# Three groups per neighbourhood step, and latent chunks begun inside the differential drain

## The chip, the cores and the metric

The kernel runs on one core of a Trainium2 chip. It is one program in which five engines work through queues of their own: TensorE (matrix products and transposes, results in PSUM), VectorE, ScalarE, GpSimd, and SyncE, which issues most transfers. They wait for each other by semaphores alone. The metric is the device time of one execution in microseconds (us).

## What is computed

The reference is two blocks, one behind the other, over 1024 tokens of width 1024. The first block has two layers of three kinds of attention each; both layers hold the code that is changed. The second block (state space mixer, stick-breaking attention, pooling, MLP) is untouched. Cut to what matters:

```python
def hybrid_layer(x, ...):                      # twice
    proj = (rms_norm(x) * (1 + scale) + shift) @ w_in
    # latent heads: 6 heads, queries and keys of 64 + 32 (rotated) from latents of 256 and 128
    q = rms_norm((rms_norm(c_q) @ w_uq)), k = rms_norm(concat(k_nope, k_pe)), rope on the last 32
    o_mla = softmax(q k^T * 96**-0.5) @ v_mla                       # 1024 x 1024 per head
    # neighbourhood heads: 6 heads of 64; tokens are a 16 x 64 grid, each sees 8 x 16 neighbours
    o_na = softmax(qn kn^T * 64**-0.5 + rpb, neighbours only) @ vn
    # differential heads: 4 heads, two score maps of 32 each
    a = softmax(q0 k0^T) - lam * softmax(q1 k1^T)
    o_d = rms_norm(a @ vd) * (1 - lam_init)
    y = concat(o_mla * silu(g_mla), o_na * silu(g_na), o_d * silu(g_diff)) @ w_out
    return x + gate * y
```

## The kernel before

A layer runs in five stages: projection, neighbourhood heads, differential heads, latent heads, output. Tokens lie along the free axis, 128 partitions hold features or, for score tiles, 128 queries. PSUM has eight banks of 512 columns, here `ps[:, 0..7]`.

**Neighbourhood stage.** 24 steps: three pairs of heads (`hp`) by eight tiles of 128 queries (`t`, `NA_PAIRS`). A step works on both heads of a pair (`j`), so unit `u` is `2 s + j`. Tiles 2 to 5 of each pair are inner ones, with 576 keys; the others have 512. TensorE forms the scores of both heads (`scores`, L1415, head 0 in banks 0 and 1, head 1 in 2 and 3). VectorE adds the bias and takes the maximum (`top`, L3160), then negates it (L3165). ScalarE exponentiates (`exps`, L2249). TensorE transposes the probabilities, four blocks of 128 keys and for inner tiles one of 64 (`probs_t`, L1429, always banks 4 and 5), ScalarE copies them out of PSUM (`evacuate`, L2259) and VectorE the block of 64 for the odd head (L3172). TensorE multiplies by the values (`values_of`, L1445, bank 6), VectorE copies the result (`out`, L3177). TensorE's order in step s is: transposes of unit 2s-1, scores of step s+1, transposes of unit 2s, values of step s-1. When a pair of heads is through, VectorE takes reciprocals of its sums (L3208), GpSimd spreads them (`na_wide`, L3833), TensorE transposes them in two halves in steps 11, 12, 19 and 20 (`factors`, L1458, bank 7), and VectorE multiplies (`out_times`, L3186). From step 10 to 19 VectorE also does one operation per step of the rotation of the latent keys (`key_rope`). In step 24 the first differential scores are formed, and then a barrier follows.

**Differential stage.** 32 units, two per tile of 128 queries. In iteration c TensorE forms the two score maps of unit c (L1477, banks 0 and 1, 2 and 3), does half of a value product (L1524, banks 6 and 7), and transposes unit c-2 (L1535, banks 4 and 5). VectorE takes maxima (L2927), a reciprocal (L3223), the difference of the two maps (L3230) and the out (L3236); ScalarE exponentiates (L2267) and copies the transposes (L2296); GpSimd forms one ratio per unit (L3844). Iterations 32 to 35 drain the pipeline. Into the drain are put four of eight latent value products (`latent_v`, L1219, copied by ScalarE, L2102), the factor transposes of the third neighbourhood pair, and the square of the first differential pair (ScalarE, L2303). Then comes a barrier (`phase_end`).

**Latent opening.** Queries and keys of a pair of heads are made in eight chunks of 256 columns (`LAT_CHUNKS`); the first six (`LAT_AHEAD`) come ahead of the first scores. A chunk goes: product on TensorE (`latent_main`, L1133 and L1136, bank p % 4), squares on ScalarE (L2060), their sum on GpSimd (`squares_sum`, L3862), sum over features on TensorE (`latent_sums`, L1143), root on ScalarE (L1895 and L1897), scaling on VectorE (`latent_scaled`, L2921 and L2955), rounding on ScalarE (L2075, L2082), low parts on VectorE (`latent_low`, L2966) and GpSimd (`turned_low`, L3869). Before the chunks TensorE makes the other four value tiles; GpSimd squares the second differential pair (L3864). Behind the chunks TensorE does the first two differential sums (L1209, L1211, banks 6 and 7), and then the first latent scores (L1160, L1167), which need chunks 0 to 4 ready and all six scaled.

The waits that hold the order around the change are these (TensorE, `latent`):

```python
pe.wait_ge(sems["lat_v_done"], NT * layer + 4 + min(p, 3) + 1)
if p >= 4:
    pe.wait_ge(sems["lat_used"], LAT_C * layer + p - 3)
latent_main(layer, p, p % 4)
if p:
    pe.wait_ge(sems["lat_v_done"], NT * layer + NT)
    if p >= 3:
        pe.wait_ge(sems["lat_rstd"], LAT_C * layer + p - 2)
    latent_sums(layer, p - 1, 4 + (p - 1) % 2, 0)
```

## Time and profile before

| | us |
|---|---|
| median of 3 timed runs (3835.05 to 3836.61) | 3835.8 |
| the profiled execution | 3830.2 |
| its span, first to last instruction | 3828.2 |
| TensorE busy | 3752.3 |
| VectorE busy | 2660.5 |
| ScalarE busy | 1927.6 |
| GpSimd busy | 643.5 |

In the profile a busy TensorE is not TensorE at its peak: matrix products are pipelined, and the row of weight loads (PEld, 2924.3 us) shows gaps that the row of products hides. "issue" is time in which an engine waited for nothing that the profile shows. The two layers take the first 1740 us or so; the two show the same pattern. A line number is that of the instruction in the kernel before.

### The profile page before, as it was taken

The numbers are of one execution on the slowest core, as the hardware profiler recorded it, in microseconds if no ns is written. First come the engines' busy times: TensorE is split into PE (matmuls) and PEld (weight loads), VectorE is DVE, ScalarE is ACT, GpSimd is POOL, SyncE is SP. The second block draws the span as 40 slices with busy tenths as digits, with TensorE's granted clock in tenths as the row PEclk, the third lists the DMA queues.
The fourth block names the chain that finished last, engine by engine and source line by source line (L and its number), as shares of the span: only waits on it lengthen the run. The fifth ranks groups of instructions, "written<-read, shape, count | busy, mean of one in ns | idle before, by whom it ended". The sixth has DMA issues, their size and how long they took to land.

```text
span 3828.2 us, 53662 instructions
## 1 busy us (share of the span) xinstructions
PE 3752.3 (98%) x21588; PEld 2924.3 (76%) x21588; DVE 2660.5 (69%) x3337; ACT 1927.6 (50%) x2841; POOL 643.5 (17%) x723
## 2 busy tenths in 40 slices
PE   8999999999999999999999999999999999999999
PEld 5876667887876667887853778888888888888887
DVE  4347967675347967534456745988889869888898
ACT  5337866324337866324357444453545554535454
POOL 0120121001120121011049911000001420000010
PEclk9999999999999999999999999999999999999999
DMA  5332000453232000332100011211121201111111
GB/s 212 94 97 54 1 1 12 176 212 108 94 97 54 1 1 13 121 118 71 45 23 1 26 45 66 78 44 44 57 76 45 77 13 67 55 44 55 67 55 66
DMA packets 67734, 247.54 MB, mean 65 GB/s; under 512 B 15648, under 2 KB 16288, under 8 KB 55456
## 3 DMA queue, kind: packets, MB, share of 16 engines
q1 hardware_dynamic: 53648, 193.51, 15.0%
q10 hardware_dynamic: 13840, 50.60, 3.6%
q8 instruction: 172, 2.82, 0.3%
q14 instruction: 74, 0.61, 0.1%
HBM read 206.34 MB, written 29.36 MB: 62 GB/s over the span
## 4 chain that ended last, share of the span: by engine, by line
PE 85%; DVE 5%; ACT 4%; issue 2%; POOL 2%; DMA 1%; DVEq 0%; SPq 0%; ACTq 0%; POOLq 0%
PE ps L1788 32%; PE ps L1045 13%; PE ps L1297 3%; PE ps L1299 3%; PE ps L1298 3%; PE ps L1477 2%; PE ps L1160 2%; PE ps L1193 2%; PE ps L1579 2%; PE ps L1524 2%; PE ps L1535 2%; PE ps L1429 2%; DMA w<-in_wstream 1%; PE ps L1445 1%; PE ps L1415 1%
## 5 line engine op out<-in xcount | busy, mean ns | idle before, releaser
L1788 PE MATMUL ps<-x_piece1hi,w_piece1hi 128*128 128x512 f32 x672 | 262.4, 390 | 0.2 <-DVE x_piece1lo L3529 0.2
L1788 PE MATMUL ps<-x_piece0hi,w_piece0hi 128*128 128x512 f32 x672 | 262.3, 390 | 0.0
L1788 PE MATMUL ps<-x_piece0hi,w_piece0lo 128*128 128x512 f32 x672 | 261.5, 389 | 0.0
L1788 PE MATMUL ps<-x_piece1hi,w_piece1lo 128*128 128x512 f32 x672 | 261.4, 389 | 0.0
L1788 PE MATMUL ps<-x_piece0lo,w_piece0hi 128*128 128x512 f32 x672 | 261.4, 389 | 0.0
L1788 PE MATMUL ps<-x_piece1lo,w_piece1hi 128*128 128x512 f32 x672 | 261.4, 389 | 0.0
L1788 PE MATMUL ps<-x_piece2hi,w_piece2lo 128*128 128x512 f32 x672 | 261.4, 389 | 0.0
L1788 PE MATMUL ps<-x_piece2hi,w_piece2hi 128*128 128x512 f32 x672 | 261.4, 389 | 0.0
L1788 PE MATMUL ps<-x_piece2lo,w_piece2hi 128*128 128x512 f32 x672 | 261.4, 389 | 0.0
L1045 PE MATMUL ps<-n_hi_m,w_lo 128*128 128x512 f32 x576 | 225.5, 391 | 0.0
L4047 POOL TENSOR_TENSOR rope_cos<-rope_cos,arena 128x512 f32<-128x512 f32 x42 | 65.4, 1557 | 730.4 <-ACT arena L2496 727.3
L2988 DVE TENSOR_REDUCE small<-ps 128x1 f32<-128x1024 f32 x96 | 113.0, 1219 | 78.7 <-PE ps L1167 78.5
L2927 DVE TENSOR_REDUCE small<-ps 128x1 f32<-128x1024 f32 x128 | 154.2, 1212 | 15.3 <-PE ps L1477 15.3
L2267 ACT ACTIVATE h<-ps,small 128x1024 f32<-128x1024 f32 x128 | 142.7, 1115 | 37.0 <-DVE small L2927 36.9
L4047 POOL TENSOR_TENSOR rope_sin<-rope_sin,arena 128x512 f32<-128x512 f32 x28 | 45.2, 1615 | 640.7 <-ACT arena L2496 638.3
L2550 ACT ACTIVATE m<-m 128x1024 f32<-128x1024 f32 x80 | 85.0, 1062 | 131.9 <-DVE m L3573 103.9
L1788 PEld LDWEIGHTS ps<-x_piece1hi,w_piece1hi 128*128 128x128 f32 x672 | 126.1, 188 | 27.2 <-DVE x_piece1lo L3529 0.6
L1788 PEld LDWEIGHTS ps<-x_piece0lo,w_piece0hi 128*128 128x128 f32 x672 | 126.1, 188 | 26.6 <-issue 0.5
L1788 PEld LDWEIGHTS ps<-x_piece1lo,w_piece1hi 128*128 128x128 f32 x672 | 126.1, 188 | 26.6 <-issue 0.5
L1788 PEld LDWEIGHTS ps<-x_piece0hi,w_piece0hi 128*128 128x128 f32 x672 | 126.1, 188 | 26.6 <-DVE w_piece1lo L3522 0.2
L1788 PEld LDWEIGHTS ps<-x_piece1hi,w_piece1lo 128*128 128x128 f32 x672 | 126.1, 188 | 26.3
L1788 PEld LDWEIGHTS ps<-x_piece0hi,w_piece0lo 128*128 128x128 f32 x672 | 126.1, 188 | 26.2
(515 smaller groups left out, 10652.3 us busy)
## 6 DMA issues: line engine op xcount, KB each, us to landing
w<-in_wstream SPq DMA_DIRECT2D x87, 1024.0 KB, 5.0
arena<-in_wstream SPq DMA_DIRECT2D x40, 1024.0 KB, 4.9
arena<-in_wstream ACTq DMA_DIRECT2D x16, 1024.0 KB, 5.3
n_saved<-n_hi_m SPq DMA_DIRECT2D x16, 512.0 KB, 7.3
n_saved<-n_lo SPq DMA_DIRECT2D x16, 512.0 KB, 8.2
n_hi_h<-n_saved SPq DMA_DIRECT2D x16, 512.0 KB, 8.2
n_lo<-n_saved SPq DMA_DIRECT2D x16, 512.0 KB, 9.2
out<-h ACTq DMA_DIRECT2D x32, 256.0 KB, 2.3
```

Of the source, the lines that this page charges most:

```text
L1045: last = mm(dst, a_part[:, k, wcols], b_part[:, tile0 + k, :], start=(k == 0 and b_part is hi and a_part is wb[0]), stop=(k == nk - 1 and ...
L1160: mm(ps[:, 2 * j + hf, :], lt_split(hp, 0, q, r)[a_part], lt_split(hp, 1, keys, r)[b_part], start=(part == 0), stop=False)
L1193: last = mm(ps[64 * j:64 * j + 64, 6, 0:P], lt_v[:, b, hp * P + 64 * j:hp * P + 64 * j + 64], lt_pt_of(2 * s + j)[:, b * P:b * P + P], sta ...
L1297: mm(dst, wb[0][:, k, wcols], hi[:, k, :], start=(step == 0), stop=False)
L1298: mm(dst, wb[0][:, k, wcols], lo[:, k, :], start=False, stop=False)
L1299: last = mm(dst, wb[1][:, k, wcols], hi[:, k, :], start=False, stop=(step == KT - 1))
L1788: last = mm(dst[:, e, :], a_part[:, pair, k, f], b_part[:, k, :], start=(n in FRESH and half == 0 and k == 0 and t == 0), stop=(half == 1 ...
L2267: nc.scalar.activation(df_p[:, 2 * (c % 3) + i, :], psf[:, 2 * i * HALF:(2 * i + 2) * HALF], ACT.Exp, bias=negm[:, e:e + 1], accum_out=sum ...
L2550: nc.scalar.activation(x, x, ACT.Square if st.kind == "up" else ACT.Sigmoid).then_inc(sems["unit_done"], 1)
L2927: V.reduce_max(negm[:, u:u + 1], src, AX.X, negate=True).then_inc(sems["m_ready"], 1)
L2988: V.reduce_max(negm[:, u:u + 1], psf[:, 2 * j * HALF:(2 * j + 2) * HALF], AX.X, negate=True)\
L4047: G.tensor_tensor(out=x, in0=x, in1=ring[:, r % 2, :], op=ALU.add).then_inc(sems["t_added"], 1)
```

## The change

In the neighbourhood stage TensorE's step becomes: scores of step s+1, transposes of both heads of step s, values of step s-1. The even head's transposes go to bank 4, the odd head's to bank 7, the 64-key blocks of both to bank 5. ScalarE copies bank 4 and the small blocks, VectorE copies bank 7. The maximum is taken negated, so that the negation goes; the exponential takes scale -1. Factors move to steps 14, 15, 22, 23 and to bank 5. The first differential scores move from step 24 to step 23.

The barrier between differential and latent stage goes. Chunks 0 to 3 and the first sums are put into iterations 32 to 35, the value products between and behind them, one bank (6) and later two (6 and 7), copied by VectorE. The squares of both differential pairs go to GpSimd, the first into its loop behind unit 20, the second between chunks 4 and 5.

```diff
@@ tiles
+        na_pt_odd, at = region(arena, lt_end + 2 * NA_INNER, NA_K)
         def df_pt_of(v):
-            return (df_pt1 if v // 2 % 2 else df_pt0)[:, v % 2, :]
+            return (df_pt0 if v // 2 % 2 else df_pt1)[:, v % 2, :]
+        LAT_SUM_PLACE = ((1, LAT_W), (1, LAT_W), (2, LAT_W), (5, 0), (4, 0), (5, 0))
+        def lat_v_bank(t):
+            return 7 if t >= 4 and t % 2 == 0 else 6
@@ SyncE, bias of the third pair
-                sp.wait_ge(sems["t_done"], 6 * layer + 2)
+                sp.wait_ge(sems["lat_rs"], 2 * LAT_PAIRS * layer + 1)
@@ TensorE, latent
             def latent_v(layer, t):
-                if t in (2, 3, 4, 5):
-                    pe.wait_ge(sems["lat_v_done"], NT * layer + t - 1)
-                mm(ps[:, t % 2 if t < 4 else t - 4, 0:384], lt_kv[:, t * P:t * P + P], lt_wv, start=True, stop=True)\
+                if t:
+                    pe.wait_ge(sems["lat_v_done"], NT * layer + (t if t < 4 else t - 1))
+                mm(ps[:, lat_v_bank(t), 0:384], lt_kv[:, t * P:t * P + P], lt_wv, start=True, stop=True)\
                     .then_inc(sems["lat_v_full"], 1)
+            def latent_opening_sums(layer, p):
+                if p == LAT_AHEAD - 1:
+                    pe.wait_ge(sems["lat_rstd"], LAT_C * layer + p - 1)
+                latent_sums(layer, p, *LAT_SUM_PLACE[p])
             def latent(layer):
-                for t in range(4, NT):
+                for p in (4, 5):
+                    pe.wait_ge(sems["lat_used"], LAT_C * layer + p - 3)
+                    latent_main(layer, p, p % 4)
+                    latent_opening_sums(layer, p - 1)
+                for t in (3, 4, 5):
                     latent_v(layer, t)
...
+                latent_opening_sums(layer, 5)
+                for t in (6, 7):
+                    latent_v(layer, t)
+                pe.wait_ge(sems["lat_v_done"], NT * layer + NT)
                 for i in range(2):
                     differential_sums(layer, i)
@@ TensorE, neighbourhood
+                    def probs_t(s):
+                        hp, t, _, inner = NA_PAIRS[s]
+                        pe.wait_ge(sems["exp_done"], T.since("exp_done", 2 * s + 2))
+                        if s:
+                            pe.wait_ge(sems["pt_act"], T.since("pt_act", s))
...
+                        for j in range(2 if inner else 0):
+                            nc.tensor.transpose(ps[0:GW, 5, j * P:j * P + P], na_p_of(2 * s + j)[:, NA_W:NA_INNER], ident)
+                        for j in range(2):
+                            if s and j:
+                                pe.wait_ge(sems["pt_dve"], T.since("pt_dve", s))
+                            for b in range(NA_W // P):
+                                last = nc.tensor.transpose(ps[:, 7 if j else 4, b * P:b * P + P],
+                                                           na_p_of(2 * s + j)[:, b * P:b * P + P], ident)
+                            last.then_inc(sems["t_full"], 1)
                     for s in range(NA_STEPS + 1):
-                        if s == NA_STEPS:
+                        if s + 1 < NA_STEPS:
+                            scores(s + 1)
+                        elif s + 1 == NA_STEPS:
...
                             for i in range(2):
                                 df_scores(0, i)
-                        if s:
-                            probs_t(2 * s - 1)
-                        if s + 1 < NA_STEPS:
-                            scores(s + 1)
-                        if s < NA_STEPS:
-                            probs_t(2 * s)
                         if s == 0:
                             keep_busy(7, 8)
+                        if s < NA_STEPS:
+                            probs_t(s)
                         if s:
                             values_of(s - 1)
-                        if s > NT and s % NT in (3, 4):
-                            factors(s // NT - 1, s % NT - 3)
+                        if s in NA_FACTORS_AT:
+                            factors(*NA_FACTORS_AT[s])
@@ TensorE, differential drain
+                        if c == U:
+                            pe.wait_ge(sems["lat_w"], 128 * (layer + 1))
+                            pe.wait_ge(sems["exp_done"], T.since("exp_done", 2 * U - 1))
+                            for p in range(2):
+                                latent_main(layer, p, p)
+                        if c == U + 1:
+                            pe.wait_ge(sems["lat_sq"], LAT_SQUARES[-1] * layer + LAT_SQUARES[1])
+                            latent_opening_sums(layer, 0)
                         if c >= 4:
...
-                        if c in (U - 1, U + 1):
-                            for v in range(2):
-                                latent_v(layer, 2 * (c > U) + v)
...
+                        if c == U + 1:
+                            pe.wait_ge(sems["na_m_done"], T.since("na_m_done", 2))
+                            for p in (2, 3):
+                                latent_main(layer, p, p)
+                            pe.wait_ge(sems["lat_rstd"], LAT_C * layer + 1)
+                            latent_opening_sums(layer, 1)
+                            pe.wait_ge(sems["o_free"], T.since("o_free", DF_STEPS - 1))
+                            latent_v(layer, 0)
+                        if c >= U + 2:
+                            latent_v(layer, c - U - 1)
+                        if c == U + 2:
+                            latent_opening_sums(layer, 2)
+                    pe.wait_ge(sems["o_free"], T.since("o_free", DF_STEPS))
-                phase_end()
@@ ScalarE
+            def latent_opening(layer, p):
+                if p < LAT_AHEAD:
+                    for part in range(2 - LAT_CHUNKS[p][1]):
+                        latent_squares(layer, p, p % 4, part)
+                if p:
+                    latent_root(layer, p - 1, *LAT_SUM_PLACE[p - 1])
+                if p >= 2:
+                    latent_high(layer, p - 2)
+                if p >= 3:
+                    turned_high(layer, p - 3)
...
+                        for j in range(2 if NA_PAIRS[s][3] else 0):
+                            nc.scalar.activation(na_pt_of(2 * s + j)[0:GW, NA_W:NA_K], ps[0:GW, 5, j * P:j * P + P], ACT.Copy)
+                        nc.scalar.activation(na_pt_of(2 * s)[:, 0:NA_W], ps[:, 4, :], ACT.Copy).then_inc(sems["pt_act"], 1)
+                    exps(0)
+                    exps(1)
+                    for s in range(NA_STEPS):
+                        evacuate(s)
+                        if s + 1 < NA_STEPS:
+                            exps(2 * s + 2)
+                            exps(2 * s + 3)
...
-                        if c in (U, U + 2):
-                            for v in range(2):
-                                latent_v(layer, 2 * (c > U) + v)
-                        if c == U + 1:
-                            act.wait_ge(sems["o_free"], T.since("o_free", NT))
-                            nc.scalar.activation(m[:, 0, :], m[:, 6, :], ACT.Square).then_inc(sems["lat_d_act"], 1)
+                        for p in {U: (0,), U + 1: (1,), U + 2: (2,)}.get(c, ()):
+                            latent_opening(layer, p)
-                phase_end()
@@ VectorE
+            def latent_v(layer, t):
+                dve.wait_ge(sems["lat_v_full"], NT * layer + t + 1)
+                V.tensor_copy(lt_v[:, t, :], ps[:, lat_v_bank(t), 0:384]).then_inc(sems["lat_v_done"], 1)
             def latent(layer):
...
+                latent_scaled(layer, 3, 3)
+                latent_v(layer, 2)
+                latent_low(layer, 2)
+                latent_scaled(layer, 4, 0)
+                latent_v(layer, 3)
+                latent_low(layer, 3)
+                latent_v(layer, 4)
+                latent_scaled(layer, 5, 1)
+                latent_low(layer, 4)
+                latent_v(layer, 5)
+                latent_low(layer, 5)
+                for t in (6, 7):
+                    latent_v(layer, t)
...
-                            na_inner[hp][:, j, :] if inner else na_bias[hp % 2][:, j, e * GW:e * GW + NA_W], 1.0, 4 * MASKED, ALU.add, ALU.max, mx[:, u:u + 1])\
-                            .then_inc(sems["v_link"], 1)
-                        dve.wait_ge(sems["v_link"], T.next("v_link"))
-                        V.tensor_scalar(negm[:, u:u + 1], mx[:, u:u + 1], -1.0, None, ALU.mult)\
+                            na_inner[hp][:, j, :] if inner else na_bias[hp % 2][:, j, e * GW:e * GW + NA_W], -1.0, -4 * MASKED, ALU.add, ALU.min, negm[:, u:u + 1])\
                             .then_inc(sems["m_ready"], 1)
+                    def probs_t(s):
+                        dve.wait_ge(sems["t_full"], T.since("t_full", 2 * s + 2))
+                        if s >= 2:
+                            dve.wait_ge(sems["o_full"], T.since("o_full", s - 1))
+                        V.tensor_copy(na_pt_of(2 * s + 1)[:, 0:NA_W], ps[:, 7, :]).then_inc(sems["pt_dve"], 1)
...
+                        if c == U + 2:
+                            latent_scaled(layer, 1, 1)
+                            latent_low(layer, 0)
+                            latent_v(layer, 0)
+                        if c == U + 3:
+                            latent_scaled(layer, 2, 2)
+                            latent_low(layer, 1)
+                            latent_v(layer, 1)
                         if c >= 5 and c % 2:
...
+                            latent_scaled(layer, 0, 0)
+                            latent_turned(layer, 0, 0)
+                            latent_turned(layer, 0, 1)
-                phase_end()
@@ GpSimd
+                    if v == DF_STEPS + 4:
+                        pool.wait_ge(sems["o_free"], (NA_STEPS + DF_STEPS + LAT_STEPS) * layer + NA_STEPS + NT)
+                        G.tensor_tensor(out=m[:, 0, :], in0=m[:, 6, :], in1=m[:, 6, :], op=ALU.mult).then_inc(sems["lat_d_sq"], 1)
+                    for p in range(2 if v == DF_U - 1 else 0):
+                        squares_sum(p)
-                phase_end()
-                G.tensor_tensor(out=m[:, 1, :], in0=m[:, 7, :], in1=m[:, 7, :], op=ALU.mult).then_inc(sems["lat_d_act"], 1)
-                for p in range(LAT_AHEAD):
+                for p in range(2, LAT_AHEAD):
                     squares_sum(p)
                     if p >= 3:
                         turned_low(p - 3)
+                    if p == LAT_AHEAD - 2:
+                        pool.wait_ge(sems["o_free"], (NA_STEPS + DF_STEPS + LAT_STEPS) * layer + NA_STEPS + DF_STEPS)
+                        G.tensor_tensor(out=m[:, 1, :], in0=m[:, 7, :], in1=m[:, 7, :], op=ALU.mult).then_inc(sems["lat_d_sq"], 1)
```

## Rows read from the trace of the kernel before

**Rows 1.** Table of stretches: us, busy by engine (instructions), granted clock, DMA share, GB/s.

```profile
484.00:513.20 29.20, 23.44 (x156) 16.89 (x152) 13.78 (x28) 17.08 (x43) 12.87 (x15) 1.00 0.00 0
1344.00:1373.50 29.50, 23.73 (x158) 17.19 (x157) 13.99 (x28) 17.37 (x44) 13.06 (x15) 1.00 0.00 1
```

**Rows 2.** Chain of waits, an inner neighbourhood step: start us, us, what.

```profile
283.98 0.70 PE ps L1429 x5
284.67 1.23 PE ps L1415 x8
285.90 0.69 PE ps L1429 x5
286.60 1.39 PE ps L1445 x20
```

**Rows 3.** Timeline, TensorE's weight loads: start us, us, engine, line, shapes, count, idle before.

```profile
480.67 0.86 PEld L1535 LDWEIGHTS ps<-mats,h 128*128 128x128 f32 x8 [0.17 <-issue]
481.58 0.94 PEld L1219 LDWEIGHTS ps<-arena 128*128 128x128 f32 x4
...
714.79 1.02 PEld L1201 LDWEIGHTS ps<-mats,arena 128*128 128x128 f32 x8
```

**Rows 4.** Chain of waits, the neighbourhood stage's second, last and next scores.

```profile
273.60 1.23 PE ps L1415 x8
...
352.78 1.06 PE ps L1415 x4
...
363.49 0.52 PE ps L1477 x3
```

**Rows 5.** Groups by shape, 268 to 362: count, busy us, mean ns, idle before.

```profile
L2259 ACT ACTIVATE h<-ps 128x512 f32<-128x512 f32 x30 | 17.9, 597 | 17.0 <-PE ps L1429 17.0
L2249 ACT ACTIVATE h<-h,small 128x576 f32<-128x576 f32 x12 | 9.2, 768 | 0.0
...
L3165 DVE TENSOR_SCALAR small<-small 128x1 f32<-128x1 f32 x48 | 7.4, 154 | 1.7
L3160 DVE CUSTOM_DVE_ANT_0 h<-ps,w 128x576 f32<-128x576 f32 x8 | 6.1, 758 | 3.4 <-PE ps L1415 2.7 <-DVE h L2937 0.7
L3172 DVE COPY h<-ps 64x128 f32<-64x128 f32 x12 | 3.4, 282 | 2.1 <-PE ps L1429 1.9
L3186 DVE TENSOR_TENSOR m<-m,ps 128x512 f32<-128x512 f32 x4 | 2.7, 687 | 1.1 <-PE ps L1458 1.1
```

**Rows 6.** Latent opening: chain pieces, timeline pieces and groups by shape of single operations.

```profile
476.44 0.34 POOL L3844 TENSOR_SCALAR small<-small,lam 128x1 f32<-128x1 f32 x1 [3.37 <-DVE small L3223]
...
492.61 2.82 PE ps L1219 x8
492.65 1.89 POOL L3864 TENSOR_TENSOR m<-m 128x1024 f32<-128x1024 f32 x1 [6.47 <-DVEq L2700]
...
504.29 0.42 DVE L2966 TENSOR_TENSOR w_lo<-w,lt_high 128x256 fp32r<-128x256 f32 x1
...
508.88 0.67 PE L1143 MATMUL ps<-h,mats_r 128*128 128x256 f32 x2 [1.06 <-POOL h L3862]
...
509.38 0.87 POOL L3869 TENSOR_TENSOR lt_high<-arena,lt_k_turned 128x256 fp32r<-128x256 f32 x1 [0.65 <-ACT lt_k_turned L2082]
509.58 0.95 DVE L2966 TENSOR_TENSOR w_lo<-w,lt_high 128x256 fp32r<-128x256 f32 x1
509.55 0.86 PE ps L1209 x2
510.00 0.42 ACT L1897 ACTIVATE h<-h 128x256 f32<-128x256 f32 x1
...
513.18 1.66 PE ps L1160 x12
...
L2966 DVE TENSOR_TENSOR w_lo<-w,lt_high 128x256 fp32r<-128x256 f32 x6 | 4.5, 756 | 0.0
L2921 DVE SCALAR_TENSOR_TENSOR w<-ps,c_tmp,h 128x256 f32<-128x256 f32 x6 | 2.9, 476 | 0.6 <-ACT h L1897 0.6
```

More of the change, by code:

```diff
@@ L510 @@
 NA_MASKS = 33 + 32
-NA_INNER_AT = [sum(x[3] for x in NA_PAIRS[:s]) for s in range(NA_STEPS + 1)]
+NA_FACTORS_AT = {NT * (hp + 1) + NT - 2 + hf: (hp, hf) for hp in range(NA_H // 2 - 1) for hf in range(2)}
 DF_UNITS = [(hp, j, t) for hp in range(DF_H // 2) for t in range(NT) for j in range(2)]
@@ L3202, in _ @@
                             top(2 * s + 3)
+                        elif s + 1 == NA_STEPS:
+                            for i in range(2):
+                                maximum(i, psf[:, 2 * i * HALF:2 * i * HALF + 2 * HALF], NA_STEPS)
+                        if s < NA_STEPS:
+                            probs_t(s)
                         if s:
@@ L3231, in _ @@
                                 .then_inc(sems["a_done"], 1)
+                        if c == U:
+                            for hf in range(H2):
+                                dve.wait_ge(sems["t_done"], T.since("t_done", hf + 1))
+                                out_times(LAT_PAIRS - 1, hf, 2 + hf)
+                        if c == U + 2:
[6 more added lines that the diff above has]
+                            latent_v(layer, 1)
                         if c >= 5 and c % 2:
@@ L3832, in na_wide @@
                 def na_wide(hp):
-                    G.tensor_copy(na_wides[hp].rearrange("p t (j d) -> p (t j) d", j=2),
-                                  rs[:, 16 * hp:16 * hp + 16].unsqueeze(2).to_broadcast([P, 16, 64])).then_inc(sems["lat_wide"], 1)
+                    for hf in range(H2):
+                        last = G.tensor_copy(na_wides[hp][hf].rearrange("p t (j d) -> p (t j) d", j=2),
+                                             rs[:, 16 * hp + 8 * hf:16 * hp + 8 * hf + 8].unsqueeze(2).to_broadcast([P, 8, 64]))
+                    last.then_inc(sems["lat_wide"], 1)
                 for hp in range(LAT_PAIRS - 1):
@@ L3839, in _, with squares_sum @@
                 phase_end()
+                def squares_sum(p):
+                    quarter = LAT_CHUNKS[p][2]
+                    pool.wait_ge(sems["lat_sq"], LAT_SQUARES[-1] * layer + LAT_SQUARES[p])
+                    x = lt_sq[:, p % 2, 0, :]
+                    other = pe_sq[:, quarter * LAT_W:quarter * LAT_W + LAT_W] if LAT_CHUNKS[p][1] else lt_sq[:, p % 2, 1, :]
+                    G.tensor_tensor(out=x, in0=x, in1=other, op=ALU.add).then_inc(sems["lat_sum"], 1)
                 pool.wait_ge(sems["lat_rs"], 2 * LAT_PAIRS * layer + LAT_PAIRS)
```

143 lines of the change are left out of this document (37 added, 106 removed).

## Prediction

> **What bounds the kernel now.** I first read the table of stretches: which engine is busy in which stage. Each of the two layers holds the same two stretches that the change touches, the neighbourhood stage (about 268 to 362 in layer 0) and the opening of the latent heads, from the last differential unit to the first latent scores (484 to 513 in layer 0, 1344 to 1373.5 in layer 1). In the opening TensorE has work for 23.4 of 29.2 us, VectorE for 13.8, ScalarE for 17.1, GpSimd for 12.9, all at the full granted clock [rows 1]: no engine is the bound, a chain across engines is. Then I read the chain of waits in the neighbourhood stage. It consists of TensorE alone, group after group without a gap: the odd head's transposes, scores, the even head's transposes, values. An inner step (576 keys; twelve of the 24) takes 0.70 + 1.23 + 0.70 + 1.39 = 4.02 us [rows 2]; an edge step (512 keys) has the same four groups without the pieces of 64 keys. So this stage gains only by what TensorE no longer does or no longer waits between groups. Last I read the weight loads, which show those gaps: a group of eight transposes loads weights for 0.86 us, and 0.17 passes before it begins after a group of another kind [rows 3].
>
> Everything is worked out for layer 0 and doubled. Sums are made against the profiled execution, 3830.2 us (span 3828.2 and 2.0 around it); the median of the timed runs is 3835.8, 5.6 above, and I lay the difference on that.
>
> **The neighbourhood step.** Four groups become three; the number of transposes stays. Two groups of four in a row pay the change of kind once: 0.17 saved. Against it stands a new wait between them, for the VectorE copy of the step before. Waits between groups of the same kind are in the trace: eight differential transposes end at 481.53 and the latent value products behind two waits start at 481.58, a gap of 0.05; the eight factor transposes at 714.79 have a wait in the middle and take 1.02 rather than 0.86 in all, of which the slow product ahead explains a part [rows 3]. The wait costs 0 to 0.16; I take 0.05, the direct gap. Saved per step 0.12, over the 21 steps from the scores at 273.60 to the last scores at 352.78 [rows 4]: 2.5 us.
>
> Does another engine become late? ScalarE now copies one head (0.60) and, in inner steps, two pieces of 64x128; the trace has no such copy on ScalarE, so I bound it between 0.2 and the 0.60 of 128x512, and take 0.2, since 0.60 is for four times the elements. VectorE copies the other head: 0.69 like the product of that size, and loses the negation, 0.15 twice, and the small copy of 0.28. VectorE's inner step is then two maxima of 0.76, a copy of 0.69 and the out, about 0.3 for as many columns as the small copy [rows 5], some 2.6 of 3.9 us, with a turning operation of 0.7 in ten steps: covered. If that cover were gone, every us would delay the next scores directly. Scale -1 in the maximum and in the exponential changes no duration.
>
> The factor transposes move from steps 11, 12, 19, 20 to 14, 15, 22, 23. A group of four costs half of the 0.86 of eight on TensorE [rows 3]. The last two now stand behind the last scores, where VectorE is late anyway (two maxima of the differential scores, the copy, two outs): 0.9 saved. The differential scores come one step earlier: from the last scores to the first differential scores behind the barrier it takes 10.7 us now [rows 4]; in the new order TensorE needs 3.9 to the differential scores, VectorE then 0.9 + 2.4 + 0.7 + 0.3, TensorE the last values 1.0, VectorE 0.6, and the barrier 0.3, together 10.1: 0.6 saved. At the start the negation leaves the way to the second scores: 0.2. Sum 2.5 + 0.9 + 0.6 + 0.2 = **4.2 us saved per layer**, between 1.9 (the wait costs 0.16) and 5.2 (nothing).
>
> **Cheap edits.** The third bias load waits for the reciprocals of step 8 rather than the factors of step 12; its three transfers go out earlier on SP's queue, and the swaps behind it wait for the end of the stage as before: 0, and were it late, the scores of head pair 2 would wait. The square of the first differential pair goes from ScalarE's drain into GpSimd's loop, 1.89 us, where GpSimd idles 3.4 us between two ratios [rows 6]: 0; above 3.4 it would hold up a differential unit one for one. The two differential tiles that change places cost nothing.
>
> **The opening.** Removed are a barrier, the ScalarE copies of eight latent value tiles, and a square on ScalarE. The copies go to VectorE: 384 columns, between 0.28 (128 columns) and 0.69 (512) [rows 5], in proportion 0.55 each. The chunks start at 481.6, when the transposes of unit 29 are through, rather than at 495. But the new queues tie the chunks together:
>
> TensorE waits for the squares of chunk 1 before the first sums. Those squares stand on ScalarE behind the copy of unit 30, so they end at 487.4; behind TensorE's wait stand the last differential values and transposes, for which ScalarE's and VectorE's copies wait. Then follow sums 0.67, values 1.02, transposes 1.02, two latent products 0.9, sums 0.67: 491.6. The root of chunk 1 (0.84) ends at 492.5.
>
> From here value tiles 1 and 2 are awaited on TensorE ahead of the sums of chunks 2 and 3, and VectorE's copy stands behind the scaling of the chunk before. A turn is scaling 0.48 + 0.42 and a handover, low part 0.42, copy 0.55, value product 0.65 (four took 2.8 with their waits), sums 0.67, root twice 0.42 [rows 6]: 4.1 us, so root 2 ends at 496.6, and root 3, with one out and one latent product more, at 501.1. Root 4 is not tied so, 502.9; root 5 waits for value tile 5 (scaling, copy, product, sums, root): 507.0. Now the last root ends at 510.4 [rows 6]. That is **3.4 us won at the last root**. Behind it, however, now stand only the differential sums on TensorE (509.55 to 513.05), which need nothing from VectorE; GpSimd's last low part ends with them. In the new order VectorE has scaling 0.95, two low parts, and three copies to do after root 5, 3.4 us, and TensorE waits for the eighth copy before the differential sums, 3.5: first scores at 507.0 + 3.4 + 3.5 + 0.1 = 514.0 against 513.2 [rows 6]: 0.8 lost.
>
> That is without collisions. A VectorE difference of two tiles took 0.42 us alone and 0.95 when GpSimd was at work, ending 0.28 behind GpSimd's own end [rows 6]. On the path above stand six of them that can meet a GpSimd operation. None meets: 0.8 lost; all: 0.8 + 6 x 0.53 = 4.0. I take three, **2.4 us lost per layer**, because in the opening of now the six low parts average 0.756, that is two thirds of them met one [rows 6]. A gain isn't excluded, since the walk holds some thirty handovers: an end of 1 us gained.
>
> The Trainium skill, page "SBUF — State Buffer", section "Who interferes with whom", states that a VectorE instruction with two SBUF inputs and a GpSimd instruction that reads SBUF exclude each other for the whole instruction. The rows above bear that out for operations of 0.9 us. By that rule the square of the second differential pair, which now stands between two chunks on GpSimd, would hold VectorE's scaling of chunk 4 for up to its 1.89 us; by the fixed 0.53 it would not.
>
> **Sum.** Per layer -4.2 + 2.4 = -1.8, both -3.6: 3826.6 for the profiled execution, 3832.2 for the median.
>
> **The rivals.** *The overlap comes through* (0.25): the drain hides the chain, the copies fall between scalings. For it speaks that chunks begin 13 us earlier; against it the order of VectorE's queue. If all of the 3.4 us at the last root stay and the copies beyond the last scaling cost nothing, the gain per layer is 4.2 + 3.4 = 7.6: 3820.6.
> *Full exclusion* (0.15): GpSimd's square between chunks, 1.89 us, holds VectorE's scaling of chunk 4, and with it value tile 5 and root 5, by 1.4 us over the 0.5 counted. Per layer -4.2 + 3.8 = -0.4: 3835.0. For it speak the rows with 0.95; against it that the square may fall where VectorE waits for a root. This is what the cited rule gives.
> *ScalarE becomes the bound in the inner steps* (0.10), the other side: transposes, copies, two exponentials, transposes form a ring. With small copies of 0.2 it takes 0.84 + 0.4 + 0.5 + 2 x 0.86 + 0.1 = 3.56, under TensorE's 3.9; it decides from 0.37 each, and at 0.55 it is 4.26. Twelve inner steps then cost 0.35 each more, 4.2 per layer; with the opening's 2.4, 2.4 slower per layer: 3840.6. Against it: no ScalarE operation in the trace takes so long for so few elements.
>
> **How the numbers follow.** The forecast (0.50) is 3832.2, its own range 3826 to 3840 (saving 1.9 to 5.2, loss 0 to 4 per layer). The first rival takes the range down to 3821; the other two lie within or at its upper end, 3840. What a measurement can tell from no change here is about 0.2%, 7.7 us: faster means under 3828.1. That is nearly all of the first rival and a sixth of the forecast: 0.33. Slower, above 3843.5, needs the third rival together with a bad opening: 0.06. The rest is 0.61.
>
> **What would show it.** Right: inner steps of 3.9 us in the chain, TensorE alone in it, and the barrier behind the neighbourhood stage 4 us earlier; in the opening TensorE idle ahead of the value products; the last root 25 to 27 us behind the transposes of unit 29 (28.9 now, 481.5 to 510.4), and 7 us or more from there to the first latent scores (2.8 now). Wrong: ScalarE in the chain of the inner steps; a step that did not shrink (the wait costs as much as the change of kind); first latent scores less than 30 us behind the transposes of unit 29 (31.7 now), which would be the overlap.

## The result, and the profile after

| | before | changed |
|---|---|---|
| time, median | 3832.1 us (20 runs, 3830.2 to 3837.5) | 3839.7 us (20 runs, 3836.1 to 3845.7) |
| profiled execution | 3830.2 us, mean granted clock 0.999 | 3840.8 us, mean granted clock 0.995 |

The ratio is 1.0018, with a 95% interval of 1.0011 to 1.0024: the changed kernel is slower by 0.18%, some 7 us. The forecast was 3832.2, a gain of 3.6 us on the median of 3835.8 that was known then. Two executions that lasted several times as long as the others, one of e8 (17155.67 us) and the profiled one of e9 (9464.05 us), are in none of the numbers below, so that e9 has no stages.

Where the time went is best read from four starts in TensorE's timeline (start us, us, engine, line, operation, tiles, count): first neighbourhood scores, first differential scores, transposes of differential unit 29, first latent scores. Of the kernel before, the first two; the other two are in [rows 3] (480.67) and [rows 6] (513.18):

```profile
265.19 0.69 PE L1415 MATMUL ps<-arena 64*128 64x512 f32 x1
...
358.72 0.49 PE L1477 MATMUL ps<-df_hi 32*128 32x512 f32 x1
```

The same four of the changed kernel, and the differential scores behind the barrier (359.85):

```profile
265.93 0.69 PE L1430 MATMUL ps<-arena 64*128 64x512 f32 x1
...
353.28 0.49 PE L1498 MATMUL ps<-df_hi 32*128 32x512 f32 x1
...
359.85 0.49 PE L1498 MATMUL ps<-df_hi 32*128 32x512 f32 x1
...
479.67 1.09 PE L1562 MATMUL ps<-mats,h 128*128 128x128 f32 x8
...
519.45 0.50 PE L1172 MATMUL ps<-lt_high 64*128 64x512 f32 x2
```

The neighbourhood stage brought what was forecast: the differential scores behind the barrier come 93.9 us after the first neighbourhood scores instead of 98.3 (363.49 in [rows 4]). Then it is lost: the transposes of unit 29 are at 213.7 instead of 215.5, and from there to the first latent scores it takes 39.8 us instead of 32.5. The chain of waits of an inner step, which answers to [rows 2], has three groups of TensorE (the pieces of 64 keys belong to the transposes) and nothing else in it:

```profile
285.14 1.23 PE ps L1430 x8
286.37 0.34 PE ps L1445 x2
286.70 0.87 PE ps L1450 x8
287.58 1.39 PE ps L1466 x20
```

That is 3.83 us instead of 4.02. The table of stretches (length; busy us of PE, PEld, DVE, ACT, POOL with counts; granted clock; DMA share; GB/s) shows what the kernel before does not have in these stages: TensorE's granted clock falls to half, 1.2 instead of 2.4 GHz, once at the changeover to the differential heads and twice in the opening of each layer. In layer 0, with the two stretches at half in the opening last:

```profile
362.00:366.00 4.00, 2.83 (x16) 1.31 (x15) 3.67 (x6) 2.76 (x5) 0.56 (x2) 0.86 1.03 257
366.00:370.00 4.00, 4.00 (x20) 2.94 (x20) 2.91 (x3) 2.97 (x5) 0.12 (x1) 0.50 1.02 223
370.00:374.00 4.00, 3.70 (x22) 2.53 (x20) 4.00 (x5) 3.24 (x5) 0.34 (x1) 0.79 1.09 216
...
484.00:500.00 16.00, 11.71 (x89) 8.58 (x90) 8.67 (x19) 6.20 (x14) 5.03 (x7) 0.94 0.00 0
500.00:512.00 12.00, 8.01 (x26) 4.77 (x24) 7.58 (x15) 5.92 (x17) 6.80 (x7) 0.93 0.00 0
512.00:520.00 8.00, 7.35 (x25) 4.55 (x26) 0.80 (x2) 1.04 (x2) 0.00 (x0) 0.60 0.01 2
...
498.00:501.40 3.40, 3.18 (x7) 2.22 (x8) 0.36 (x2) 0.39 (x1) 0.18 (x1) 0.50 0.00 0
511.60:518.40 6.80, 6.15 (x14) 3.21 (x13) 1.20 (x3) 0.60 (x1) 0.00 (x0) 0.50 0.01 2
```

The clock column of [rows 1] was 1.00. What half the clock costs is seen in the timeline of the opening: the value products (L1231) wait for VectorE's copies (L3027), the one at 498.22 then runs for 1.65 instead of 0.91 us, and the differential sums (L1221, L1223) last 6.3 us, from 513.20 to 519.45, instead of 3.6 (509.55 to 513.18 in [rows 6]):

```profile
498.22 1.65 PE L1231 MATMUL ps<-arena 128*128 128x384 f32 x2 [2.21 <-DVE arena L3027]
499.66 1.06 PE L1145 MATMUL ps<-arena,h 128*128 128x256 f32 x2
500.51 1.03 PE L1155 MATMUL ps<-h,mats_r 128*128 128x256 f32 x2
...
506.81 0.91 PE L1231 MATMUL ps<-arena 128*128 128x384 f32 x2 [1.34 <-DVE arena L3027]
...
511.24 1.31 PE L1231 MATMUL ps<-arena 128*128 128x384 f32 x2 [2.44 <-DVE arena L3027]
513.20 2.07 PE L1221 MATMUL ps<-m,mats_r 128*128 128x512 f32 x2 [0.65 <-DVE arena L3027]
515.07 1.91 PE L1223 MATMUL ps<-mats,arena 128*128 128x128 f32 x8
516.77 1.86 PE L1221 MATMUL ps<-m,mats_r 128*128 128x512 f32 x2
518.47 1.05 PE L1223 MATMUL ps<-mats,arena 128*128 128x128 f32 x8
```

### The profile page after: what moved, and what is told of

Its sections match the earlier page's. It is cut to its first block, busy times and chain, and to the rows that moved or that the text cites. A ratio compares the mean times of both kernels' runs of the same rounds, so it can differ in the third digit from the quotient of the medians.

```text
span 3839.0 us, 53494 instructions
## 1 busy us (share of the span) xinstructions
PE 3756.3 (98%) x21588; PEld 2933.7 (76%) x21588; DVE 2677.4 (70%) x3281; ACT 1898.8 (49%) x2823; POOL 646.0 (17%) x731
## 4 chain that ended last, share of the span: by engine, by line
PE 84%; DVE 6%; ACT 4%; issue 3%; POOL 2%; DMA 1%; DVEq 0%; ACTq 0%; POOLq 0%
PE ps L1821 31%; PE ps L1057 13%; PE ps L1312 3%; PE ps L1314 3%; PE ps L1313 3%; PE ps L1498 2%; PE ps L1172 2%; PE ps L1205 2%; PE ps L1612 2%; PE ps L1562 2%; PE ps L1466 1%; PE ps L1551 1%; PE ps L1430 1%; PE ps L1190 1%; PE ps L1450 1%
```

## The experiments

All stages are between the starts shown above: A from the first neighbourhood scores to the first differential scores, B from there to the transposes of unit 29, C from there to the first latent scores; us, layer 0 / layer 1 where they differ by more than 0.05.

| kernel | A | B | C | ratio to before (95%) |
|---|---|---|---|---|
| before | 93.53 | 121.95 | 32.51 | 1 |
| changed | 87.35 | 126.39 / 125.90 | 39.78 / 38.39 | 1.0018 (1.0011 to 1.0024) |
| e1 filler at the changeover | 87.37 | 125.33 | 39.81 / 38.22 | 1.0012 (1.0003 to 1.0021) |
| e2 filler in the opening | 87.37 | 124.74 | 35.32 | 1.0004 (0.9995 to 1.0013) |
| e3 new neighbourhood alone | 87.37 | 123.75 | 32.52 | 0.9974 (0.9963 to 0.9985) |
| e4 new opening alone | 93.53 | 122.97 | 36.94 / 39.80 | 1.0038 (1.0024 to 1.0052) |
| e5 product reordered | 87.35 | 126.23 / 128.77 | 37.86 / 38.21 | 1.0012 (1.0003 to 1.0021) |
| e6 e2, square on ScalarE | 87.38 | 123.82 / 124.99 | 35.42 | 0.9997 (0.9988 to 1.0006) |
| e7 e3, filler moved | 85.90 | 125.35 / 127.74 | 32.52 | 0.9979 (0.9970 to 0.9988) |
| e8 e7, filler at the changeover | 85.91 | 124.27 | 32.51 | 0.9969 (0.9958 to 0.9981) |
| e9 filler and order | – | – | – | 0.9990 (0.9981 to 0.9999) |
| e10 every repair | 85.90 | 124.36 / 128.44 | 34.33 | 0.9981 (0.9972 to 0.9990) |
| e11 e10, second square on ScalarE | 85.89 | 124.36 | 34.10 | 0.9976 (0.9967 to 0.9985) |
| e12 e11, copies on ScalarE | 85.90 | 124.36 | 32.93 | 0.9971 (0.9959 to 0.9982) |

The first differential scores of the new schedule stand one step earlier, ahead of 6.6 us of work to the barrier instead of 4.8, so 1.8 us have gone from A to B: A and B together are 215.48 before and 211.12 in e3.

**e1, filler at the changeover** (`keep_busy(bank, n)` is n matmuls of 128x384 into a bank not in use, whose result nobody reads; the kernel before already has 8 of them ahead of the third differential scores).

```
+ if s == NA_STEPS - 1: keep_busy(4, 3)     # ahead of the last values
- keep_busy(4, 8)                           # third differential scores
+ keep_busy(4, 1 if i else 12)              # and their second half
```

> The changed kernel with filler matmuls (128x384, 0.21 us each) where TensorE idles between the neighbourhood and the differential heads: 3 ahead of the last values, 12 instead of 8 ahead of the third differential scores, 1 ahead of their second half. Theory 1 (TensorE's granted clock): the changed kernel shows 0.50 from 366 to 370 us, which costs 2.6 us a layer; with the gaps filled the clock stays at 1.00, the differential scores take 0.9 us again instead of 1.4 to 1.6, and the transposes of unit 29 lie 3.5 us ahead of the kernel before instead of 0.9, about 5 us in all: ratio to the kernel before 1.0005 instead of 1.0018. Theory 2 (the dip is of no account because VectorE bounds the differential steps anyway): the transposes of unit 29 stay at 0.9 us ahead and the ratio stays at 1.0018.

The clock stayed at 1.00 at the changeover of both layers, and B fell by 1.1 and 0.6 us, less than expected: the filler is itself in the way by 0.6 (e2, without it and without a dip, has 124.7). The transposes of unit 29 (477.23) lie 3.4 us ahead of before, near theory 1's 3.5, and 2.4 ahead of the changed kernel; but 1.4 of these come from a stage that began earlier. The ratio went the expected way, but its interval overlaps that of the changed kernel.

**e2, filler in the opening:** 7, 10, 6, 11 and 3 matmuls ahead of value products 1, 2, 5, 7 and of the differential sums, into bank 4; those of product 5 first wait for root 4.

> The changed kernel with filler matmuls in the waits for the value copies of the latent opening (7 ahead of the second value product, 10 ahead of the third, 6 ahead of the sixth, 11 ahead of the eighth, 3 ahead of the differential sums). Theory 1 (clock): the clock stays near 1.00 from 492 to 520 us, the two differential sums ahead of the first latent scores take 3.5 us instead of 6.3, the products and sums about 500 us another 1.3 us less; from the transposes of unit 29 to the first latent scores 34.5 us instead of 38.8; about 8 us in all, ratio 0.9998. Theory 2 (the chain through VectorE's queue is what is long, and the clock only shows it): the differential sums shorten by at most 2.8 us, the value products wait as long as before, and it is 36 us or more; ratio 1.0004 or above. Theory 3 (port collisions of VectorE and GpSimd): the stretch loses nothing but the differential sums, and the low parts stay at 0.9 us.

Theory 1 in the trace: the clock is 1.00 throughout the opening, and the differential sums last 3.7 us again (507.82 to 511.51):

```profile
484.00:500.00 16.00, 15.41 (x101) 11.58 (x98) 9.48 (x22) 7.98 (x23) 6.71 (x8) 1.00 0.00 1
500.00:512.00 12.00, 11.04 (x54) 7.99 (x54) 6.29 (x12) 3.41 (x9) 4.20 (x5) 1.00 0.00 0
...
507.82 1.12 PE L1222 MATMUL ps<-m,mats_r 128*128 128x512 f32 x2
508.78 1.05 PE L1224 MATMUL ps<-mats,arena 128*128 128x128 f32 x8
509.67 1.02 PE L1222 MATMUL ps<-m,mats_r 128*128 128x512 f32 x2
510.53 1.05 PE L1224 MATMUL ps<-mats,arena 128*128 128x128 f32 x8
511.51 0.50 PE L1173 MATMUL ps<-lt_high 64*128 64x512 f32 x2
```

C is 35.3 in both layers: 4.5 and 3.1 us less than in the changed kernel, for 37 matmuls that compute nothing. That is 0.8 more than theory 1 said, and the ratio, 1.0004, is theory 2's, with theory 1's 0.9998 inside its interval. The low parts of theory 3 stay as they were in the changed kernel (0.95, 0.95, 0.48, 0.48, 0.89 and 0.65 us). C is still 2.8 above the 32.5 of before; that is what the walk itself, from chunk to chunk across the engines, costs.

**e3, the new neighbourhood schedule alone, and e4, the new opening alone:** the diff applied by halves.

> The new neighbourhood schedule with the old way into the latent heads (barrier, value copies on ScalarE). Theory 1: the barrier lies 3.6 us earlier a layer as in the changed kernel; the clock falls to 0.50 behind it as there and takes 2.6 us a layer back, so that 0.9 us a layer is left and the total is 2 us below the kernel before (0.9995). Theory 2 (the dip is an accident of that one profile or hidden): 7 us below (0.9982).

> The old neighbourhood schedule with the new way into the latent heads. Theory 1: the clock is 1.00 through the differential heads, falls to half in the opening, and the first latent scores come 38.8 us behind the transposes of unit 29 (31.7 in the kernel before), 7 us a layer: total 9 to 14 us above the kernel before (1.0024 to 1.0037). Theory 2 (what the changed kernel loses lies in the neighbourhood half): no more than 2.4 us a layer, 1.0013 or below.

e3 shows what the new neighbourhood stage was worth: 9.8 us between the medians, more than the 7 of the second theory, whose 0.9982 lies within the interval. A and B together lose 4.36 us, C stays. The expected dip did not come, though the code of the changeover is that of the changed kernel, so the dip there is not in the code alone:

```profile
360.00:364.00 4.00, 2.84 (x19) 1.63 (x18) 4.00 (x7) 2.45 (x5) 0.34 (x1) 1.00 1.00 255
364.00:368.00 4.00, 3.38 (x26) 2.21 (x25) 4.00 (x5) 3.79 (x6) 0.68 (x2) 1.00 1.02 224
```

e4 is 13.9 us slower (3845.4 against 3831.5), as theory 1 had it: with the new opening the clock falls in C here too, and is 1.00 in A and B of both layers. It also shows a second loss: B is 1.0 longer than before, with the old schedule.

**That 1.0 us** is in the changed kernel's timeline. The square of the first differential pair was put on GpSimd, beside VectorE's combination of a unit (L3260, 1.28 us each time, here once in a layer 2.33):

```profile
436.97 1.28 DVE L3260 SCALAR_TENSOR_TENSOR h<-h,small 128x1024 f32<-128x1024 f32 x1
...
440.30 1.89 POOL L3898 TENSOR_TENSOR m<-m 128x1024 f32<-128x1024 f32 x1
...
440.94 2.33 DVE L3260 SCALAR_TENSOR_TENSOR h<-h,small 128x1024 f32<-128x1024 f32 x1
```

**e6** takes it away from e2 (the differential sums there wait for both squares from the first on):

```
- G.tensor_tensor(out=m[:, 0, :], in0=m[:, 6, :], in1=m[:, 6, :], op=ALU.mult)
+ nc.scalar.activation(m[:, 0, :], m[:, 6, :], ACT.Square)   # differential step 22
```

> The kernel with the filler in the opening, and the square of the first differential pair on ScalarE in differential step 22 (1.0 us there) instead of on GpSimd in its step 20. Theory 1 (exclusion): the VectorE combination of the step that met the square takes 1.28 us again instead of 2.33, and the differential heads from their first scores to the transposes of unit 29 take 123.7 us instead of 124.7; ratio 1.0 us a layer better than with the filler alone, 0.9999. Theory 2 (ScalarE has no room, or the step had slack): 124.7 us or more, ratio 1.0004.

Theory 1: the step that met it takes 1.28 us, the square 1.05 on ScalarE, and B in layer 0 is 123.8 instead of 124.7, as in e3. In layer 1 the clock fell to 0.58 from 1226 to 1230 us and took it back. The Trainium skill, page "SBUF — State Buffer", section "Who interferes with whom", states that a VectorE instruction with two inputs in SBUF and a GpSimd instruction that reads SBUF exclude each other for the whole instruction; the trace agrees within 0.2 us: the combination, 1.28 us alone, ends 1.08 us behind the end of the square, at 443.27.

**e5, the order on TensorE:** value product 2 from ahead of the products of chunk 4 to behind the sums of chunk 3.

> The changed kernel with one value product (tile 2) moved on TensorE from ahead of the products of chunk 4 to behind the sums of chunk 3; nothing else, no filler. Theory 1 (the walk is long because work of a chunk waits on TensorE behind a value product that waits for a copy which stands on VectorE behind the scaling of the chunk before): the products of chunk 4 come directly behind the last differential values, 3.6 us earlier than now, root 3 about 3 us earlier, and the first latent scores about 3 us earlier if the clock is the same: 36 to 37 us behind the transposes of unit 29; ratio to the kernel before 1.0003. Theory 2 (VectorE's work behind the last root and its meetings with GpSimd set the end): root 3 earlier, but the first latent scores less than 1 us; ratio 1.0015 or above.

Theory 1 failed as put. The products of chunk 4 came 1.3 us earlier behind the transposes of unit 29, not 3.6: they lost one wait and met the next, the copy of the last differential output, which stands on VectorE behind the whole chain of chunk 2:

```profile
497.28 1.22 PE L1145 MATMUL ps<-arena,h 128*128 128x256 f32 x2 [2.41 <-DVE m L3280]
```

The clock fell here as in the changed kernel, so that C (37.9 and 38.2) says little; the ratio is not told apart from the changed kernel's.

**e9, the order with the output copy put ahead, and filler (27 matmuls, at places that fit the new order); e10, every repair at once; e11, the second square on ScalarE; e12, also the last three value copies on ScalarE and the sums of chunk 5 ahead of value product 5.**

> The changed kernel with filler in the opening, the value product of tile 2 behind the sums of chunk 3, and on VectorE the copy of the last differential output ahead of the scaling of chunk 2 instead of behind its chain (the run with the order alone showed the products of chunk 4 waiting 2.4 us for that copy). Theory 1 (work of a chunk queued behind another chunk's chain is what makes the walk long): the products of chunk 4 come within 1 us of the last differential values, 3 us earlier than with the filler alone; transposes of unit 29 to first latent scores 32.3 us instead of 35.3; ratio 0.9990. Theory 2 (VectorE's tail of copies and low parts sets the end): 34.5 us or more, ratio 1.0002.

> The changed kernel with every repair: filler in the opening and at both ends of the neighbourhood stage, value product and output copy reordered, the first pair's square on ScalarE. Theory 1 (the three causes, clock, GpSimd's square and the queue order, account for all of the loss, and add): 85.9 + 124.0 + 32.3 = 242.2 us a layer from the first neighbourhood scores to the first latent scores against 248.0 in the kernel before, 11.6 us in all: 0.9970. Theory 2 (they overlap, or something else is lost): 245 us a layer or more, 0.9984 or above.

> The kernel with every repair, and the square of the second differential pair on ScalarE too (behind root 4) instead of on GpSimd between two chunks (2.08 us there). Theory 1 (full exclusion of VectorE by that square, as the second rival of the prediction had it): the scaling of chunk 4, 0.65 in the kernel with every repair and 1.05 with the filler alone, takes 0.42, and from the transposes of unit 29 to the first latent scores 33.3 us or less instead of 34.3. Theory 2 (the square falls where VectorE waits anyway): 34.0 us or more.

> As the run before, and the sums of chunk 5 on TensorE ahead of the value product of tile 5, with the last three value copies on ScalarE. Theory 1 (the queue of copies and scalings on VectorE sets the end of the opening): root 5 about 2 us earlier, the differential sums directly behind the last copies, 32 us or less from the transposes of unit 29 to the first latent scores, under the 32.5 of the kernel before: only then is the overlap worth anything; ratio 0.9965. Theory 2 (GpSimd's low parts and the walk of the chunks keep the end): 33.3 us or more, 0.9978.

e9's ratio fits its first theory; the size is read from e10's trace, which has the same opening at a clock of 1.00. First e2, then e10, the products of chunk 4 and root 5:

```profile
495.51 0.59 PE L1146 MATMUL ps<-arena,h 128*128 128x256 f32 x2
...
503.60 0.42 ACT L1935 ACTIVATE h<-h 128x256 f32<-128x256 f32 x1
```

```profile
492.95 0.70 PE L1146 MATMUL ps<-arena,h 128*128 128x256 f32 x2 [0.39 <-DVE m L3287]
...
502.54 0.42 ACT L1940 ACTIVATE h<-h 128x256 f32<-128x256 f32 x1
```

Counted from the start of the transposes of unit 29 (476.20 and 476.12), the products of chunk 4 came 2.5 us earlier than in e2, the end of root 5 only 1.0; from there to the first latent scores it is 7.5 us in both, and C is 34.33, 1.0 less. So 1.5 us of what was won was lost again ahead of root 5: value product 2 and its wait now stand in front of the products of chunk 5, which came 0.6 us earlier; no run takes this apart. By its number the second theory is the nearer one; its reason, VectorE's tail, is not shown, for the tail did not change.

e10 as a whole: layer 0 has 244.6 us for A, B and C, between the two theories, layer 1 a dip of the clock in spite of the filler. In e11 the scaling of chunk 4 took 0.42 instead of 0.65 us, and C fell by the same 0.2 us: theory 2 by the number. In e12 root 5 came 0.8 us later (I had put a copy ahead of it on ScalarE), but the copies came earlier, and C is 32.9, between the theories. So with every repair the overlapped opening is still 0.4 us longer than the old one with its barrier (32.5), and the ratio is not told apart from that of e8, which has no overlap.

**e7 and e8, the start of the stage and the changeover**, on top of e3:

```
- if s == 0: keep_busy(7, 8)
  if s < NA_STEPS: probs_t(s)
+ if s == 0: keep_busy(5, 2)
```

> The new neighbourhood schedule alone with the old way into the latent heads, and with the filler of the first step (8 matmuls, 1.6 us) moved behind the first transposes and cut to 2. In the new order ScalarE's copy for step 0 stands ahead of the exponentials of step 1, and that copy waits for transposes that stand behind the filler. Theory 1: transposes of step 1 come 1.3 us earlier; the stage from the first scores to the first differential scores takes 86.1 us instead of 87.4; ratio 0.9967 instead of 0.9974. Theory 2 (the start is set by the transfers of the biases or by the clock): 87.4 us, 0.9974.

> The new neighbourhood schedule alone, with the filler of its first step behind the transposes and cut to 2, and filler at the changeover to the differential heads (3 matmuls ahead of the last values, 11 instead of 8 ahead of the third differential scores). The same kernel without the filler at the changeover had the neighbourhood stage at 85.9 us instead of 87.4, but a granted clock of 0.5 to 0.6 behind it and so 125.4 and 127.7 us of differential heads instead of 123.7. Theory 1 (clock): with the filler the clock is 1.00 from 358 to 374 us, the differential heads take 124.0 us or less, and the time is 1.3 us a layer under the new schedule alone: 0.9968. Theory 2 (the heads wait for the transfers of that stretch or for VectorE, whatever the clock): 125 us or more, 0.9975 or above.

e7's A fell by 1.5 us as expected, and its ratio did not: the clock fell at the changeover in both layers. e8 has the filler there (3 and 11 matmuls), the clock is whole in both layers, and B is 124.3, a little above the 124.0 of its theory 1. First e7, then e8:

```profile
362.00:366.00 4.00, 4.00 (x20) 2.85 (x22) 3.46 (x4) 2.55 (x5) 0.34 (x1) 0.53 1.03 228
366.00:370.00 4.00, 3.93 (x24) 2.79 (x22) 3.12 (x4) 2.64 (x4) 0.34 (x1) 0.62 1.12 238
```

```profile
362.00:366.00 4.00, 3.17 (x22) 2.04 (x24) 4.00 (x6) 2.87 (x7) 0.34 (x1) 1.00 1.01 241
366.00:370.00 4.00, 3.46 (x26) 2.08 (x24) 4.00 (x5) 3.79 (x6) 0.34 (x1) 1.00 1.04 238
```

At 0.9969, e8 has the lowest ratio of the study, by the ratios 12 us under the kernel before and 19 under the changed one. Its interval overlaps those of e3, e7, e10, e11 and e12, so none of these is shown to be the best.

## Why the prediction was wrong, point by point

**The neighbourhood stage: right.** 4.4 us a layer (98.3 to 93.9) against 4.2, an inner step of 3.83 against 3.9, TensorE alone in the chain. Its terms were off and cancelled: in the chain of waits, from the scores at 277.02 to the last scores it took 75.76 before and 71.45 now (277.84 to 349.29), 4.3 where the steps and the moved factors were to give 3.4, for an inner step lost 0.19, as if the new inner wait cost nothing; tail and start, forecast at 0.8, gave 0.1. The chain before was not TensorE's alone throughout, as the prediction had read it: at one factor step, from 318.2 to 319.8, it ran through VectorE. And the scores at 273.60, called the second in [rows 4], are the third, as the 21 steps have it. At the start ScalarE's copy of step 0 stands ahead of the exponentials of step 1 and waits for transposes behind the filler, a queue that I had not followed; e7 took 1.5 us out of it. The rival of a ScalarE ring is dead: ScalarE is in no chain of an inner step, and its small copies took 0.26 to 0.27 us, where 0.37 was to decide.

**The square of the first pair: the step that costed it at 0 failed.** I asked whether GpSimd had room for it, and it had; I did not ask what VectorE does beside it, although the cited rule stood further down, for the other square. It cost 1.05 us a layer. The rival of full exclusion had the right mechanism at the wrong square: the scaling of chunk 4 met only the last 0.8 us of the second one and was held in e2 for 0.6 (1.05 for 0.42), not for up to 1.9; in e10, where the order is another, taking it away gave 0.2:

```profile
498.93 2.07 POOL L3927 TENSOR_TENSOR m<-m 128x1024 f32<-128x1024 f32 x1
...
500.23 1.05 DVE L2986 TENSOR_TENSOR arena<-arena,h 128x256 f32<-128x256 f32 x1
```

**The opening: the walk was right, at full clock.** In e2 roots 1 to 5 end 10.6, 15.2, 20.2, 22.5 and 26.8 us behind the end of the transposes of unit 29 (the forecast, without collisions: 11.0, 15.1, 19.6, 21.4 and 25.5; for the last 25 to 27 with them), the last 7.5 us ahead of the first latent scores (forecast 7 or more); C is 2.8 longer than before, the forecast 2.4. The rival in which the overlap comes through is dead: no repair got C under 32.5, where that rival needed 29.1.

**TensorE's clock: not in the sum at all, and this is the step that turned a gain into a loss.** The forecast read the full clock in [rows 1] and carried it over to a stage that it filled with waits; it named waits of TensorE ahead of value products and gave them the price of the wait. The price of what follows at half the clock is larger: C of the changed kernel less C of e2 is 4.5 and 3.1 us, B less B of e2 1.7 and 1.2. The clock's own rows fit: in the opening it was at half for 10.2 us of layer 0 and 6.8 of layer 1 (1364.9 to 1368.3 and 1378.6 to 1382.0), and if all of that work took twice its time, half of it is lost, 5.1 and 3.4. By layers, layer 0: -4.4 (neighbourhood) + 1.0 (square) + 2.8 (walk) + 1.7 + 4.5 (clock) = +5.6; layer 1: -4.4 + 1.0 + 2.8 + 1.2 + 3.1 = +3.7; together +9.3 of the 10.6 us by which the two profiled executions differ. These terms are steps of one path, from the kernel before over e3 and e2 to the changed one, so that they add up to the measured difference of A, B and C by construction; what bears them out singly are e4 (B +1.0), e6 and the rows of the clock. Without the clock it would have been -0.6 a layer; with the square at its place, -1.4 in e6's layer 0, near the -1.8 of the forecast.

**The base: the step that laid 5.6 us on the median failed too.** The median of 20 runs is 3832.1, not 3835.8; from there the same -3.6 would have given 3828.5. That the measured 3839.7 lies inside the stated 3826 to 3840 is therefore luck: from the true base the same savings and losses give 3822 to 3836, and it lies outside. The 5.6 us go with the clock: of the 27 runs of the kernel before taken beside e5, fifteen with a mean granted clock of 0.999 average 3830.7 us, eleven with 0.997 average 3835.7. The profiled execution is of the first kind, the three runs that I had, 3835.05 to 3836.61, are by their times of the second. No execution of the second kind was profiled, so where its clock falls is not shown. The changed kernel shows 0.994 to 0.997 in its 20 runs, and its time follows: 3843.6 at 0.994, 3837.3 at 0.997. That the profiled execution lay 5.6 us from three runs that agree within 1.6 was a row to be read before the sum.

**What stays open** is what makes the clock fall. With the new opening it fell in eight of eight layers without filler in it, and in none of ten with it; with the old opening in none of eight. At the changeover, with the new schedule, it fell in seven of twelve without filler and in one of ten with it. But idle time alone doesn't tell these apart: in the old opening of e3 TensorE was busy for 1.80 of the 4 us from 500 to 504 at a clock of 1.00, and e3 and the changed kernel have the same changeover, with the same idle times of 0.7, 0.9 and 0.2 us, one whole, the other at half; the kernel before has them there too, at full clock. It also fell where nothing was changed (at 1092 us in e2, between 3051 and 3076 in e1, e4 and e12), so the mean clock of a run doesn't say which stage was at half. Which activity counts, and why the same code dips in one execution and not in the next, was not tried.

## What to carry to other kernels

Where a change makes TensorE wait in short pieces in a stage that had none, price the work that follows at either clock, and look at the mean granted clock of the runs that you have: times that go with it warn that the clock may fall in this kernel. When an operation moves to GpSimd because there is room, read what VectorE does at that time, not only the gap it goes into. And split a change that both shortens a stage and overlaps the next: here the one half was worth 10 us and the other cost 14.

## What the runs showed of the hardware that was not expected

- In the changed kernel TensorE's granted clock fell from 2.4 to 1.2 GHz in stretches where it never idled for more than 2.44 us at once (opening) or 0.94 us (changeover); in e2, 37 matmuls of 0.21 us that compute nothing gave back 3.1 to 4.5 us a layer in the opening.
- The filler is no guarantee: e10 has it at the changeover, and in layer 1 its clock was 0.50 from 1222 to 1230 us and fell once more at 1239, with B 4.1 us longer than in layer 0.
- A GpSimd square of 1.89 us with two SBUF reads stretched a VectorE operation of 1.28 us with two SBUF inputs to 2.33, and the differential stage of each layer by 1.0 us.
